# Expert input rows selected by one-hot matrix products on TensorE instead of fetched from DRAM

## The reference

```python
top_v, top_i = lax.top_k(e_logits, TOP_K)                 # 2 of 32 experts for each token
xb = x_pad[slot_tok].reshape(n_blocks, MOE_BLOCK, D)      # rows of h, put in the order of the experts
def expert_block(args):
    xblk, e = args
    hid = jax.nn.silu(xblk @ w_gate[e]) * (xblk @ w_up[e])
    return hid @ w_down[e]
```

## Time and profile before

| | us |
|---|---|
| median of 3 runs | 3775.41 (3772.46 to 3776.14) |
| the profiled execution, its time | 3775.55 |
| the profiled execution, its span in the profile | 3773.8 |
| TensorE busy | 3470.4 (92%) |
| VectorE, ScalarE, GpSimd busy | 1477.2, 568.5, 486.6 |
| first product of the experts starts at | 1243.65 |
| last product of the experts ends at | 2220.29 |

### The profile page before, as it was taken

How to read it: one execution, slowest core, us unless ns; L and a number is a source line. 1 busy time by engine, 2 the same in 40 slices (tenths; PEclk the granted TensorE clock), 3 DMA queues, 4 the chain that set the end, 5 groups by cost and what they waited for, 6 DMA issues and landing times.

```text
span 3773.8 us, 51395 instructions
## 1 busy us (share of the span) xinstructions
PE 3470.4 (92%) x21663; PEld 2354.9 (62%) x21663; DVE 1477.2 (39%) x2536; ACT 568.5 (15%) x1089; POOL 486.6 (13%) x440
## 2 busy tenths in 40 slices
PE   7999999999999877777777759999999999999999
PEld 5887777776545322232322228744588888888888
DVE  4557677776413200000000024572133363454532
ACT  2223222222203000000000013201100000331000
POOL 1410110100000000000000000032000001465511
PEclk9999999999999999999999989999999999999999
DMA  3222121114034899999999986245233322223432
GB/s 109 80 57 65 45 62 50 53 52 141 32 134 164 345 421 422 422 422 421 421 420 419 419 294 157 80 111 118 88 112 112 112 71 86 79 90 117 152 105 73
DMA packets 322845, 672.81 MB, mean 178 GB/s; under 512 B 43276, under 2 KB 228022, under 8 KB 269781
## 3 DMA queue, kind: packets, MB, share of 16 engines
q1 hardware_dynamic: 313877, 639.50, 46.7%
q0 software_dynamic: 8768, 30.42, 2.2%
HBM read 639.58 MB, written 47.05 MB: 182 GB/s over the span
## 4 chain that ended last, share of the span: by engine, by line
PE 41%; SPq 23%; issue 1%; DMA 1%; DVE 1%; ACT 0%; POOLq 0%; POOL 0%; DVEq 0%; ACTq 0%
SPq L2196 23%; PE stream_bank L2785 20%; PE stream_bank L2690 7%; PE stream_bank L3442 5%; PE stream_bank L2688 2%; PE experts_run_bank L2242 1%; PE stream_bank L3243 1%; DMA whole_big<-in_expert_w_down 1%; PE stream_bank L3330 1%; PE stream_bank L3306 1%; PE experts_run_bank L2262 0%; PE stream_bank L2574 0%; PE stream_bank L3317 0%; ACT whole_big L2556 0%; PE stream_bank L3295 0%
## 5 line engine op out<-in xcount | busy, mean ns | idle before, releaser
L2785 PE MATMUL stream_bank<-whole_big 128*128 128x256 f32 x3584 | 783.5, 380 | 0.6 <-DVE whole_big L3909 0.6
L2785 PEld LDWEIGHTS stream_bank<-whole_big 128*128 128x128 f32 x3584 | 679.4, 190 | 97.3 <-issue 3.7
L2242 PE MATMUL experts_run_bank<-whole_big 128*64 128x512 f32 x2048 | 486.1, 620 | 174.5 <-DMA whole_big<-in_expert_w_gate 100.5
L332 PE MATMUL first_bank<-whole_big 128*128 128x256 f32 x2240 | 538.8, 390 | 0.0
L2242 PEld LDWEIGHTS experts_run_bank<-whole_big 128*64 128x64 f32 x2048 | 169.2, 142 | 490.0 <-issue 489.9
L332 PEld LDWEIGHTS first_bank<-whole_big 128*128 128x128 f32 x2240 | 414.7, 191 | 90.4 <-issue 30.1
L2836 DVE TENSOR_TENSOR whole_big<-stream_bank,whole_big 128x256 f32<-128x256 f32 x292 | 119.5, 422 | 428.9 <-PE stream_bank L2785 428.8
L2690 PE MATMUL stream_bank<-whole_big 128*128 128x512 f32 x640 | 278.8, 594 | 0.0
L2307 DVE TENSOR_TENSOR whole_big<-whole_big,experts_run_bank 128x512 f32<-128x512 f32 x16 | 11.0, 688 | 643.6 <-PE experts_run_bank L2242 643.6
L2262 PE MATMUL experts_run_bank<-whole_big 128*64 128x512 f32 x1024 | 230.0, 596 | 35.2 <-DMA whole_big<-in_expert_w_down 22.7
L2690 PEld LDWEIGHTS stream_bank<-whole_big 128*128 128x128 f32 x640 | 120.2, 190 | 145.5 <-issue 145.0
(11 more groups left out here) (483 smaller groups left out, 3672.7 us busy)
## 6 DMA issues: line engine op xcount, KB each, us to landing
whole_big<-in_expert_w_gate SPq DMA_DIRECT2D x128, 1024.0 KB, 26.8
whole_big<-in_expert_w_up SPq DMA_DIRECT2D x128, 1024.0 KB, 29.7
whole_big<-in_expert_w_down SPq DMA_DIRECT2D x128, 1024.0 KB, 26.6
whole_big<-in_w_in SPq DMA_DIRECT2D x110, 1024.0 KB, 5.8
whole_big<-in_w_out SPq DMA_DIRECT2D x16, 1024.0 KB, 7.3
whole_big<-in_w_out SPq DMA_DIRECT2D x8, 2048.0 KB, 12.9
gates_two<-whole_big SPq DMA_DIRECT2D x40, 256.0 KB, 8.0
whole_big<-gates_two POOLq DMA_DIRECT2D x40, 256.0 KB, 3.0
```

Source lines behind the costliest of these rows:

```text
L332: mm = pe.matmul(self.place(m), weights[:, k, :], left[:, k, :], start=(k == 0), stop=(k == 7))
L2242: mm = pe.matmul(bank[self.half(h), :], self.x_T[:, PARTS * q + k, self.half(h)], self.ring[slot][:, k, :], start=(q == 0 and k == 0), sto ...
L2785: mm = pe.matmul(self.place[m % 3], weights[:, k, :], left[:, k, :], start=(k == 0), stop=(k == self.k - 1))
```

## The change

For pairs 1 to 15 the rows are no longer gathered from DRAM and transposed. Pair 0 still is. VectorE makes a matrix of zeros and ones over tokens and slots (`mark`), with the inverse root mean square in place of the one, and TensorE multiplies the rows on chip by it (`select`). The product comes out already transposed, as `turn` leaves it, and sums over 4 tiles of tokens. The stationary operand is every fourth column of the rows, `block[:, k, :]`, 128 columns 4 floats apart, and the streamed one is the one-hot matrix of 128 columns.

```diff
+    def select(self, pe, n, rows):
+
+        pe.wait_ge(self.hot_made, n)
+        for q in range(4):
+            if q >= 2:
+                pe.wait_ge(self.x_ready, 4 * n + q - 1)
+            for k in range(PARTS):
+                for t in range(TT):
+                    block = rows[:, t, q * T:(q + 1) * T].rearrange("s (p k) -> s k p", k=PARTS)
+                    mm = pe.matmul(self.x_bank[q % 2][:, k * P:(k + 1) * P], block[:, k, :], self.hot[:, t, :],
+                                   start=(t == 0), stop=(t == TT - 1))
+            mm.then_inc(self.turned, 1)
+
+    def mark(self, dve, n, middle):
+
+        code, place, inv = middle.code, middle.place_no, middle.inv
+        done = 6 * n - 6
+        dve.wait_ge(self.turned, 4 * n)
+        dve.tensor_scalar(code[:, :, :], code[:, :, :], float(PAIR_STEP), None, ALU.subtract).then_inc(self.hot_step, 1)
+        dve.wait_ge(self.hot_step, done + 1)
+        dve.tensor_tensor(self.hot[:, :, :], place.unsqueeze(1).broadcast_to([P, TT, P]),
+                          code[:, :, 0:1].broadcast_to([P, TT, P]), ALU.is_equal).then_inc(self.hot_step, 1)
+        dve.wait_ge(self.hot_step, done + 2)
+        for t in range(TT):
+            dve.scalar_tensor_tensor(out=self.hot[:, t, :], in0=place, scalar=code[:, t, 1:2], in1=self.hot[:, t, :],
+                                     op0=ALU.is_equal, op1=ALU.add).then_inc(self.hot_step, 1)
+        dve.wait_ge(self.hot_step, done + 6)
+        dve.tensor_tensor(self.hot[:, :, :], self.hot[:, :, :], inv.unsqueeze(2).broadcast_to([P, TT, P]),
+                          ALU.mult).then_inc(self.hot_made, 1)
...
@@ place(t), for each tile of tokens
+            do(stt(out=self.code[:, t, :], in0=self.pair[:, t, :], scalar=float(PAIR_STEP), in1=self.spot[:, t, :],
+                   op0=ALU.mult, op1=ALU.add))
...
@@ GpSimd, in the loop
-                        if not (last and b):
-                            pool.wait_ge(x.turned, 4 * n + 4)
-                            x.gather(pool, bass.ds(n + 1, 1), n + 1)
                         x.scatter(pool, bass.ds(n, 1), n)
...
@@ TensorE, in the loop
-                        x.turn(pe, 2 * i + 1)
+                        x.select(pe, 2 * i + 1, middle.rows)
...
@@ VectorE
                 x.take_x(dve, 0)
+                x.mark(dve, 1, middle)
...
                         if not (last and b):
                             x.take_x(dve, 2 * i + b + 1)
+                        if not last:
+                            x.mark(dve, 2 * i + b + 2, middle)
                         x.put_y(dve, 2 * i + b, place(i, b), (2, 3), first=(first and b == 0))
```

More of the change, by code:

```diff
@@ L1765 @@
 SKIP = 1 << 20
+PAIR_STEP = 4096
 PARTS = 4
@@ L1791, in __init__ @@
         self.hot, self.both, self.hot_rank = take(TT, 2, E), take(TT, E), take(2, E)
-        self.rank, self.spot = take(TT, 2), take(TT, 2)
+        self.rank, self.spot, self.code = take(TT, 2), take(TT, 2), take(TT, 2)
         self.slots_from = small.at
@@ L2166, in __init__ @@
         self.x_T, self.silu, self.hidden, self.hidden_T = region.take(KD, P), region.take(T), region.take(T), region.take(KF, P)
+        hot_at = region.at
         region.at = KD * T // 2
         self.x, self.y = region.take(D), region.take(D)
+        self.hot = big[:, MIX_AT + hot_at:MIX_AT + hot_at + TT * P].rearrange("p (t s) -> p t s", t=TT)
+        assert hot_at + TT * P <= KD * T // 2
         self.arrived = [s.sem(f"arrived{i}") for i in range(RING)]
@@ L2348, in experts @@
         run = Overflow(s, bank[3])
+        x.hot_made, x.hot_step = s.sem("hot_made"), s.sem("hot_step")
         turns = PAIRS // 2
@@ L2420, in turn_next @@
                             pe.wait_ge(run.over_done, 1)
-                        x.turn(pe, 2 * i + 1)
+                        x.select(pe, 2 * i + 1, middle.rows)
                     x.products(pe, 2 * i, place(i, 0), turn_next)
-                    x.products(pe, 2 * i + 1, place(i, 1), None if last else lambda: x.turn(pe, 2 * i + 2))
+                    x.products(pe, 2 * i + 1, place(i, 1), None if last else lambda: x.select(pe, 2 * i + 2, middle.rows))
                 x.turn(pe, 0)
```

## The result

| | before | after |
|---|---|---|
| median of the runs | 3773.93 us (3770.2 to 3776.14) | 3934.26 us (3930.38 to 3935.9) |
| span of the profiled execution | 3773.8 us | 3928.6 us |
| TensorE busy | 3470.4 us (92%) | 3826.7 us (97%) |
| the experts, first product to last | 976.6 us | 1135.8 us |

The changed kernel is slower: ratio 1.0425, 95% interval 1.0412 to 1.0437, or 160.3 us. The forecast was 3900 us, 123 us more than before (range 3832 to 3945).

What follows compares the result with a forecast made beforehand. DMA bytes bound the experts' stage; with select at 27.5 us a pair TensorE would bind it, making the gathers' 18.9 us worthless. The stage grows 123 us: 3775.5 + 123 = 3899, rounded to 3900 us, range 3832 to 3945.

Steps and rivals of the forecast that it cites:

- The bound: Experts' stage: DMA bytes set 61 us a pair before, TensorE could give 15.4; after the change TensorE binds.
- The gathers' gain: Experts' stage: 15 gathers removed, 7.9 MB or 18.9 us while DMA binds, worth nothing once TensorE does.
- VectorE, nothing: mark adds some 3 us a pair on VectorE, covered by put_y's wait of 15.5 us; counted as nothing.
- The clock: TensorE's granted clock in the experts' stage: 0.96 before, expected nearer 1.00 after the change.
- The price of a record: select on TensorE: stepped weight load sets the pace, 0.214 us for each of 128 records, 27.5 us a select.
- the forecast's own: Range of kernel time for select paces from 0.20 to 0.23 us: 3873 to 3931 us, chance 0.62.
- The upper bound: select's pace if load and streaming follow each other: 0.214 + 0.055 = 0.27 us a record, 4007 us.
- A: Rival in select: the step costs a product nothing, the stage stays bound by bytes, 3757 us; chance 0.16.
- B: Rival in select: step adds fixed 70 ns a load, 0.182 us a record, 3837 us; 0.14 with paces 0.15 to 0.20.
- C: Rival in select: granted clock falls as the array streams half the time, 55 us more, 3955 us; chance 0.08.
- D: Rival on VectorE: mark delays put_y and so the scatter; worth nothing here, no chance of its own given.
- The sum: Experts' stage: 42.9 + 27.5 = 70.4 us a pair for 15 pairs, last pair 43.8, total 1099.8 us against 976.6.

Runs made afterwards that it cites:

- the first experiment: The changed kernel with select reading 128 channels side by side instead of every fourth as its stationary operand; 3752.2 us, ratio to before 0.9941.

## Why the prediction came out as it did

**The bound.** Right. The bytes set the stage before, and the idle time of TensorE, 15.4 us a pair, was what could be given away. The gathers' gain is there where the bytes bind (25 us, forecast 18.9) and gone where TensorE does, by the two experiments that put them back.

**VectorE, nothing.** Right: `mark` alone is a ratio of 1.0000, in the kernel before.

**The clock.** Right for this kernel: the clock stayed at 1.00 through `select`. Behind a `select` that streams half as much, the down products pay for the lower clock.

**The price of a record.** The mechanism was right: the load of 128 stationary columns sets the pace, and a step about doubles it (0.112 to 0.234 us). The size was off, and this is the step of the sum that carries the whole miss. I took 0.214 us from L3278, whose columns are 128 floats apart, in preference to doubling; measured is 0.234. `select` takes 30.0 us and not 27.5: 2.5 us in 15 pairs are 37 us, and 160.3 - 37 = 123 us is the forecast. The bounds of 0.112 and 0.27 us held it, but 0.234 lies just above the 0.20 to 0.23 us that had most of the chances: 3934 us is in the stated range and 3 us outside the forecast's own (3873 to 3931).

Two terms inside the 0.214 were off, in opposite directions. The load grew by more than the 102 ns taken from L3278: 138 ns, to 330 ns where I expected one near 290. L3278's step is a long one, and the step of 16 costs less than the step of 4 too (28.05 us a `select`, 0.219 us a record); that the one explains the other is likely, not shown. The better reading for the load was the ratio in L2226, which has the very step of the change, 129 / 59 = 2.2: 82 + 2.2 x 110 = 324 ns. But the longer load does not go straight into the pace, as I had it: of the 138 ns, 122 show up there. With 324 ns and that rule the pace would have been 0.244 us, 20 us too much in the kernel's time instead of 37 too little. The two errors of 0.214 cancelled in part, and so far its nearness is luck. The upper bound had an error too: 0.055 us for streaming 128 columns is half of what a record takes, since 256 columns go at 0.218 us each and 128 at half of that, 0.109. It had no effect, as the two do not follow each other.

**The rivals.** A, the step costs nothing, is what the first experiment does: 3752 us, where I had 3757 for it. It is not this kernel. B, a fixed 70 ns, is out: 138 ns were added to the load and 122 to the pace. C showed only where 64 columns were streamed. D was nothing.

**The sum.** 42.9 us for a pair without the turning holds: 72.8 - 30.0 = 42.8. The last pair took 43.8, as forecast.

## What to carry to other kernels

Look at how the stationary operand of a float32 product lies before counting columns: here a step of 4 floats or more made the load of 128 columns 1.6 to 1.7 times as long and about doubled the pace of products of 128 columns, which the load sets. Try which operand can be stationary: exchanging the two turned 160 us of loss into 19 us of gain. And before work is moved from a saturated resource to an idle one, hold its price against the idle time of that one: here 15.4 us a pair, of which contiguous columns would have used 12 and those with a step asked for 27.

## What the runs showed that I had not expected

- The load of 128 stationary float32 columns costs 110, 114, 180, 248, 253 and 230 ns above a fixed 82 with a step of 1, 2, 3, 4, 8 and 16 floats.
- The same load sets the same pace at either level of the clock (0.235 and 0.234 us with 64 streamed columns), and it is the products behind it that lose by the lower one.
- With 64 instead of 128 streamed columns in each record of 0.234 us, the granted clock over the stage was 0.80 and not 1.00, though TensorE's busy time reads 841 of 850 us. A busy engine in the profile is no promise of the full clock.
- With the gate and up weights in pieces of 2, 4 and 8 KB and the down weights in pieces of 8 KB, the stage moved 398, 414 and 422 GB/s with all 16 DMA engines busy; where only the 2 KB pieces ran, 387.
- A float32 record of 512 columns with 128 stationary ones takes 0.43 us; with 64 stationary columns in each half of the array, side by side, one record goes by every 0.22 us.
